# A two-layer decoder trunk on eight cores: all loads of x go through the queue of the weights, and the mixing of three token groups stands before the last two arrive

## The chip, the cores and the metric

The kernel runs on the 8 cores of one Trainium2 chip, each with its own share of the batch: one prompt of 2048 tokens and 16 running sequences with 8 new tokens each, so 2176 tokens of width 1024 a core. No core waits for another. The metric is the device time of the slowest core, in microseconds.

## The reference

```python
def trunk(x, c, pool_buf, ...):
    for i in range(DEPTH):                               # 2 layers
        sh1, sc1, g1, sh2, sc2, g2 = ada_modulation(c, w_ada[i], b_ada[i])   # silu(c) @ w_ada + b_ada
        h = modulate(x, norm_g[i, 0], sh1, sc1)          # rms_norm(x, g) * (1 + sc) + sh
        if i % N_MIXERS == 0:
            y, nb = pool_mixer(h, buf, pos0, w_pool[j], pool_scale[j])
        else:
            y, vr = sgu_mixer(h, ...)
        x = x + g1 * y
        h = modulate(x, norm_g[i, 1], sh2, sc2)
        x = x + g2 * channel_mlp(h, mlp_w1[i], mlp_w2[i])   # relu(h @ w1)**2 @ w2, width 4096
    return rms_norm(x, final_g), ...
```

The pool mixer takes, for each of four groups of 256 channels, the mean over the last 2, 4, 8 or 16 tokens less the token itself, and multiplies it by the group's 256x256 matrix. Layer 0 is a pool layer, layer 1 a gating layer.

## The kernel before

Tokens are the free dimension and channels the partitions: xT_sb holds all of x in float32 as 8 chunks of 128 channels, hT_sb the normed input in bf16. Tokens go in five groups GR of 384, 512, 512, 384 and 384; the last 128 are the running sequences. In the text x0 to x4 are the loads of these groups, 4096 bytes for each token, 8.9 MB in all.

Weights come as pieces of 2 MB of float32 in HBM, written as 1 MB of bf16 into a ring of NRING = 6 slots, in the order of the list PIECES. "ada a" is the piece of 512 columns of w_ada of layer 0: a = 2, 3 the scale of the mixer, 4, 5 its gate, 8, 9 and 6, 7 scale and shift of the MLP, 10, 11 its gate, 0, 1 the shift of the mixer. The piece wpool is 1 MB, written as float32. Pieces are issued on the queue of GpSimd (POOL), one after the other (load_piece, L545; the DMA is L558, for wpool L554). A piece waits for a free slot: until the last reader of the piece before it in the slot is done. Two pieces wait for a load of x too (GATE, L543): the first one for x2, ada 8 for x4. The loads of x are issued on SP's queue (load_x, L520).

The steps at the start, for a group g: pool_z (L713) takes the squares (ScalarE, L618), sums them over channels by a matmul with ones (L621), makes the reciprocal root (L632, L635), and multiplies x by it into hT_sb (z_ops, VectorE, L643). pool_P (L730) makes the sums over 4, 8 and 16 tokens for the upper channels. pool_mm (L759) multiplies (L793): 48 matmuls of the group's width, and the residual goes into xT_sb (resid, L690), which needs ada 4 and 5. The weights of this product are w_pool times the scale of the mixer, in two versions: 16 copies on ScalarE (L822) into a ring slot of their own, wA, which is held until the last pool_mm. They need wpool and ada 2 and 3. h2_prompt (L835) makes the second norm of the group, and affine (L647) applies scale and shift (ada 8, 9, 6, 7). ada_piece (L575) is 32 matmuls of 17 columns and an addition on VectorE (L590). Then mlp(0) starts: for each block of 512 hidden units mm1 (L951, with w1) and mm2 (L977, with w2) over the five groups. The running sequences are mixed within block 0 (sample_pool, L852).

The order of instructions on each engine is not that of the text. A planner (Sched, L88) collects all operations with a cost and a priority (S.base, or S.clk, which advances by the cost of matmuls) and places one at a time: of each engine's ready operations the one of lowest priority value that can start first, and of the engines the earliest:

```python
cands.sort(key=lambda c: (c[0], c[1]))   # time, then the engine's place in
ENGS = ("pe", "act", "dve", "pool", "sp")
```

It keeps a time for the DMA engines (DMA_RATE, DMA_LAT), in which loads follow each other. "after" orders two operations in the plan without a wait on the chip. A ring slot is given to the operation that is placed first. On the chip each engine runs its list in the planned order and waits on semaphores.

Of the kernel before, what the change touches and what calls it, by code (L numbers as in the profile page):

```python
# [18 lines left out]
GR = [(0, 384), (384, 512), (896, 512), (1408, 384), (1792, 384)]  # L19
# [4 lines left out]

ENGS = ("pe", "act", "dve", "pool", "sp")
LAT = {"pe": 0.16, "act": 0.28, "dve": 0.24, "pool": 0.3, "sp": 0.3}
DMA_RATE = 300.0e3
DMA_LAT = 2.2
TABLE_BIAS = 2.5

PIECES = [("ada", 0, a) for a in (2, 3)] + [("wpool", 0, 0)] + [("ada", 0, a) for a in (4, 5, 8, 9, 6, 7)] \
    + [("w1", 0, 0), ("ada", 0, 10), ("ada", 0, 11), ("w2", 0, 0), ("ada", 0, 0), ("ada", 0, 1)]
for _b in range(1, 8):
    PIECES += [("w1", 0, _b), ("w2", 0, _b)] + [("ada", 1, a) for a in range(2 * (_b - 1), min(12, 2 * _b))]
PIECES += [(w, 1, h) for w in ("inu", "inv", "out") for h in range(2)]
PIECES += [(w, 1, b) for b in range(8) for w in ("w1", "w2")]
# [363 lines left out]
def build_program():  # L400
    nc = bass.Bass("TRN2", target_bir_lowering=False)
    S = Sched(nc)
# [76 lines left out]
    def vcol(c, n=1):  # L479
        return vecs.ap()[:, c:c + n]  # L480
# [18 lines left out]
    def MK(l, v, dc0=0, n=8):  # L499
        return (("modT", l, v), dc0, dc0 + n)  # L500

    def hb(g):
        return GR[g][0] + 16 * (g + 1)
# [4 lines left out]
    def XK(t0, t1, dcs=range(8)):  # L508
        return [(("xT", dc), t0, t1) for dc in dcs]
# [7 lines left out]
    S.op("dve", lambda e: e.memset(hT.ap()[:, :, 0:16], 0.0), writes=HK(0, 16), cost=0.3)  # L517
    xoff = [8 * t0 for (t0, n) in GR]

    def load_x(g, after=()):  # L520
        t0, n = GR[g]
        S.op("sp", lambda e: e.dma_start(
            out=xT.ap()[:, :, t0:t0 + n], in_=d_xp.ap()[:, 8 * t0:8 * t0 + 8 * n].rearrange("p (c t) -> p c t", t=n)),
            writes=XK(t0, t0 + n), stream="s_x%d" % g, cost=0.1, nbytes=4096 * n, after=after)

    for g in range(3):
        load_x(g)
    S.op("act", lambda e: e.activation(out=siluT.ap(), in_=vcol(VCT, 136).rearrange("p (a b) -> p a b", b=NSEQ), func=AF.Silu),
         reads=VR, writes=[("siluT", 0, 1)], table="silu", cost=0.4)
    S.op("dve", lambda e: e.tensor_scalar(out=vcol(VFG, 8), in0=vcol(VFG, 8), scalar1=float(np.sqrt(D)), scalar2=None, op0=ALU.mult),  # L530
         reads=VR, writes=VR)
    S.op("dve", lambda e: e.tensor_scalar(out=vcol(VN, 32), in0=vcol(VN, 32), scalar1=float(np.sqrt(D)), scalar2=None, op0=ALU.mult),
         reads=VR, writes=VR)
# [3 lines left out]


    piece_vb = {}
    prev = [None]  # L540
    S.base = -5.0

    GATE = {("ada", 0, 2): 2, ("ada", 0, 8): 4}  # L543

    def load_piece(i):  # L545
        key = PIECES[i]
        v = S.vb("ring")
        piece_vb[key] = v
        gate = []
        if key in GATE:  # L550
            t0, n = GR[GATE[key]]
            gate = XK(t0, t0 + n)
        if key[0] == "wpool":
            n = S.op("pool", lambda e, v=v: e.dma_start(out=ring[v.slot].ap().bitcast(F32), in_=d_wp.ap()),  # L554
                     writes=[(v.key, 0, 1)], stream="w%d" % i, cost=0.53, vbs=[v], nbytes=1 << 20,
                     after=[prev[0]] if prev[0] is not None else [])
        else:
            n = S.op("pool", lambda e, v=v, i=i: e.dma_start(out=ring[v.slot].ap(), in_=d_wpk.ap()[i]),  # L558
                     reads=gate, writes=[(v.key, 0, 1)], stream="w%d" % i, cost=0.53, vbs=[v], nbytes=1 << 21,
                     after=[prev[0]] if prev[0] is not None else [])  # L560
        prev[0] = n

# [2 lines left out]
    def load_upto(key):  # L565
        k = PIECES.index(key)
        while nloaded[0] <= k:
            load_piece(nloaded[0])
            nloaded[0] += 1
# [5 lines left out]
    def ada_piece(l, a):  # L575
        key = ("ada", l, a)
        load_upto(key)
        pvb = piece_vb[key]
        v = S.vb("ps")
        mms = []  # L580
        for jj in range(4):
            for dc in range(NDC):
                mms.append((lambda e, jj=jj, dc=dc: e.matmul(  # L583
                    P_(v)[:, jj * 32:jj * 32 + NSEQ], pv(key, 512)[:, dc, jj * 128:(jj + 1) * 128], siluT.ap()[:, dc, :],
                    start=(dc == 0), stop=(dc == NDC - 1)), [(pvb.key, 0, 1), ("siluT", 0, 1)], NSEQ))
        ch = S.chain(mms, v, vbs=[pvb])
        vi, dc0 = (a * 4) // 8, (a * 4) % 8
        dst = modT.ap()[:, l, vi, dc0:dc0 + 4, :]
        bb = vcol(VBA + l * 48 + a * 4, 4)
        ev = S.op("dve", lambda e: e.tensor_tensor(  # L590
            out=dst, in0=P_(v)[:, 0:128].rearrange("p (a b) -> p a b", b=32)[:, :, 0:NSEQ], in1=bcast(bb, [1, 4], [0, NSEQ]), op=ALU.add),
            reads=[(v.key, 0, 1)] + VR, writes=[MK(l, vi, dc0, 4)], cost=0.3, vbs=[v])
        S.evac(ch, ev)
        gcol = None
        if vi in (1, 4):
            gcol = vcol(VN + (l * 2 + (0 if vi == 1 else 1)) * 8 + dc0, 4)
        elif vi == 2 and l == 0:
            gcol = vcol(VPS + dc0, 4)
        if gcol is not None:
            S.op("dve", lambda e: e.tensor_tensor(out=dst, in0=dst, in1=bcast(gcol, [1, 4], [0, NSEQ]), op=ALU.mult),  # L600
                 reads=[MK(l, vi, dc0, 4)] + VR, writes=[MK(l, vi, dc0, 4)], cost=0.3)

    sqi = [0]

# [154 lines left out]
    def pool_mm(g):  # L759
# [6 lines left out]
        for dco in range(NDC):  # L766
# [30 lines left out]
            for nd in resid(0, 2, v, dco, t0, n, 0, 0):  # L797
                S.evac(ch, nd)

    for a in (2, 3):  # L800
        S.base = 34.0
        ada_piece(0, a)
    load_upto(("ada", 0, 5))
    S.base = -5.0
    load_x(3, after=[prev[0]])
    load_x(4, after=[prev[0]])
    for g in range(5):
        S.base = [5.0, 12.0, 20.0, 53.0, 62.0][g]
        pool_z(g)
    S.base = 14.0  # L810
    pool_P(0)
    S.base = 25.0
    pool_P(1)
    S.base = 26.0
    wpv = piece_vb[("wpool", 0, 0)]
    Ap = bcast(modT.ap()[:, 0, 1, 0, 0:1], [NSEQ, 8])
    for q in range(2):
        S.op("dve", lambda e, q=q: e.tensor_tensor(out=Aw.ap()[:, q * 8:q * 8 + 8], in0=Ap, in1=vcol(VCW + 8 * q, 8), op=ALU.mult),
             reads=[MK(0, 1)] + VR, writes=[("Aw", q, q + 1)], cost=0.17)
    for k in range(8):  # L820
        for q in range(2):
# [3 lines left out]
                scale=Aw.ap()[:, q * 8 + k:q * 8 + k + 1]),  # L825
                reads=[(wpv.key, 0, 1), ("Aw", q, q + 1)], writes=[(wAvb.key, q * 8 + k, q * 8 + k + 1)],
                cost=c_act(256), vbs=[wpv, wAvb])
    for a in (4, 5):
        S.base = 50.0
        ada_piece(0, a)  # L830
    for a in (8, 9, 6, 7):
        S.base = 70.0
        ada_piece(0, a)

    def h2_prompt(g, base):  # L835
        t0, n = GP[g]
        S.base = base
        R, RK = stats(t0, n)
        z_ops(hb(g), t0, n, R, RK)
        affine(0, 1, hb(g), n, "act" if g < 3 else "dve")  # L840

    cl = [51.0, 60.0, 70.0, 80.0, 90.0]
    for g in range(5):
        S.base = cl[g]
        pool_mm(g)
        h2_prompt(g, cl[g] + 3.0)
        if g + 2 < 5:
            S.base = cl[g] + 4.0
            pool_P(g + 2)


    def sample_pool():  # L852
# [6 lines left out]
        H4 = arB(HH, 8 * 16 * 23).rearrange("p (c b j) -> p c b j", c=8, j=23)  # L859
        S.op("pool", lambda e: e.dma_start(out=arB(HH, 2944), in_=d_spT.ap()),  # L860
             writes=[AR(HH, HH + 5888)], stream="s_sp", cost=0.53, nbytes=1507328)
        S.base = 120.0
        for a in (0, 1):
            ada_piece(0, a)

# [1 line left out]
             reads=[("zl", 0, 1), MK(0, 1)], writes=[("zl", 0, 1)], cost=0.35)  # L867
# [480 lines left out]
```

How the kernel before makes its waits and increments, by code:

```python
                def body(eng, ops=seq[e], e=e):  # L351
                    for n in ops:
                        ins = None
                        for (emit, w) in n.swaits:
                            for d in w:
                                eng.wait_ge(d.sigval[0], d.sigval[1])
                            ins = emit(eng)
                        if n.stream is not None:
                            ins.then_inc(n.sigval[0], 16)
                        elif n.sig:
                            ins.then_inc(n.sigval[0], 1)
                    if e == "sp":
                        for (sem, val) in final:
                            eng.wait_ge(sem, val)
                        for e2 in ENGS:
                            if e2 != e and cnt[e2] > 0:
                                eng.wait_ge(esem[e2], cnt[e2])
```

## Time and profile before

| | |
|---|---|
| time, median of 3 runs | 1322.47 us (1322.31 to 1326.92) |
| the profiled execution | 1323.73 us, span of its slowest core 1322.2 us |
| spans of the 8 cores | 1315.9 to 1322.2 us |
| TensorE busy | 1255.1 us (95%) |
| VectorE busy | 765.4 us (58%) |
| VectorE's residual step (L690), 728 in all | 638 ns each on average |
| ScalarE busy | 587.5 us (44%) |
| DMA, mean over the span | 69 GB/s written on chip, 145.43 MB read from HBM |

Busy time is the time in which an instruction of the engine runs. Times in the trace count from the first instruction of the core. Matmuls overlap: one of 384 columns shows as 326 ns, while the next one starts half as long after it, so the pace is read from groups of them. All rows are of core 3, the slowest.

### The profile page before, as it was taken

How to read it: one execution, taken by the hardware profiler on the slowest of the kernel's cores; microseconds unless marked ns; L12 is line 12 of the kernel's file. 1: busy time of each engine (PE TensorE's matmuls, PEld its weight loads, DVE VectorE, ACT ScalarE, POOL GpSimd, SP SyncE). 2: the span in 40 equal slices, each digit the busy share in tenths (PEclk: the TensorE clock that was granted, in tenths of full speed). 3: DMA queues.
4: the chain of work that ended last, by engine and by line, in shares of the span. 5: the costliest groups of instructions: out<-in, count | busy, mean ns of one | idle time of the engine just before them, and what ended most of it. 6: DMA issues, size and time to landing. Idle time of an engine off the chain costs nothing.

```text
span 1322.2 us, 21660 instructions; the slowest of 8 cores (1315.9 to 1322.2 us)
## 1 busy us (share of the span) xinstructions
PE 1255.1 (95%) x7558; PEld 670.3 (51%) x7558; DVE 765.4 (58%) x1478; ACT 587.5 (44%) x1088; POOL 45.2 (3%) x87
## 2 busy tenths in 40 slices
PE   3299999999999999999999999999999999999995
PEld 0156565555555555555444444554545555554543
DVE  4287856545445454577657657854545445454567
ACT  5349443433333333466443555533333333333474
POOL 0001000000000000000000000000000000000000
PEclk9999999999999999999999999999999999999998
DMA  9999936434243342502000016511303031100024
GB/s 256 193 151 171 152 53 118 92 63 96 52 78 65 64 80 49 96 1 45 20 1 1 1 32 120 105 33 32 59 7 64 1 64 29 36 1 0 1 108 164
DMA packets 23880, 91.08 MB, mean 69 GB/s; under 512 B 2768, under 2 KB 10192, under 8 KB 15696
## 3 DMA queue, kind: packets, MB, share of 16 engines
q0 software_dynamic: 9392, 67.34, 28.7%
q1 hardware_dynamic: 14384, 22.35, 5.6%
q8 instruction: 65, 1.06, 0.3%
q14 instruction: 39, 0.32, 0.1%
HBM read 145.43 MB, written 11.01 MB: 118 GB/s over the span
## 4 chain that ended last, share of the span: by engine, by line
PE 89%; DMA 5%; ACT 2%; DVE 2%; issue 1%; POOL 0%; SPq 0%; DVEq 0%; ACTq 0%; POOLq 0%
PE ps L977 35%; PE ps L951 34%; PE ps L1126 5%; PE ps L1097 4%; PE ps L1213 4%; PE ps L793 2%; DMA ring<-w_pack 2%; PE ps L621 2%; DMA xT_sb<-x_pack 2%; ACT hT_sb L653 1%; PE ps L583 1%; PE ps L1128 1%; DVE xT_sb L1253 1%; DMA arena<-ln_b 1%; PE ps L1179 1%
## 5 line engine op out<-in xcount | busy, mean ns | idle before, releaser
L690 DVE SCALAR_TENSOR_TENSOR xT_sb<-ps,modT,xT_sb 128x512 f32<-128x512 f32 (+3 forms) x728 | 459.0, 638 | 440.5 <-PE ps L977 393.5
L977 PE MATMUL ps<-arena,ring 128*128 128x384 bf16 (+3 forms) x2624 | 521.7, 343 | 0.1
L951 PE MATMUL ps<-hT_sb,ring 128*128 128x384 bf16 (+2 forms) x2592 | 519.7, 345 | 0.0
L957 ACT ACTIVATE arena<-ps 128x384 bf16<-128x384 f32 (+3 forms) x324 | 169.6, 527 | 497.4 <-PE ps L951 497.3
L977 PEld LDWEIGHTS ps<-arena,ring 128*128 128x128 bf16 x2624 | 253.9, 98 | 215.6 <-issue 0.6
L951 PEld LDWEIGHTS ps<-hT_sb,ring 128*128 128x128 bf16 x2592 | 251.2, 98 | 216.2
L959 ACT ACTIVATE arena<-arena 128x384 bf16<-128x384 bf16 (+3 forms) x324 | 180.6, 561 | 28.8 <-ACT arena L957 2.2
L618 ACT ACTIVATE sq<-xT_sb 128x384 bf16<-128x384 f32 (+3 forms) x216 | 105.8, 530 | 72.1 <-DVE xT_sb L690 42.1
L643 DVE TENSOR_TENSOR hT_sb<-xT_sb,rstd 128x768 bf16<-128x768 f32 (+2 forms) x80 | 75.4, 1005 | 38.9 <-ACT rstd L635 38.8
L621 PE MATMUL ps<-sq,ones 128*128 128x384 bf16 (+3 forms) x216 | 49.0, 355 | 23.0 <-ACT sq L618 20.9
L1126 PE MATMUL ps<-ring,hT_sb 128*128 128x512 bf16 x272 | 67.2, 392 | 2.6 <-ACT arena L1102 2.6
L558 POOL DMA_DIRECT2D ring<-w_pack x62 | 33.6, 542 | 925.9 <-PE ps L951 335.2
L1097 PE MATMUL ps<-hT_sb,ring 128*128 128x384 bf16 (+1 forms) x320 | 61.3, 347 | 0.0
L1213 PE MATMUL ps<-arena,ring 128*128 128x384 bf16 (+1 forms) x320 | 60.0, 347 | 0.0
L583 PE MATMUL ps<-siluT,ring 128*128 128x17 bf16 x768 | 23.1, 172 | 26.8 <-DMA ring<-w_pack 26.5
L1213 PEld LDWEIGHTS ps<-arena,ring 128*128 128x128 bf16 x320 | 31.0, 98 | 27.8 <-issue 0.7
L1097 PEld LDWEIGHTS ps<-hT_sb,ring 128*128 128x128 bf16 x320 | 31.0, 98 | 27.4 <-issue 0.7
L621 PEld LDWEIGHTS ps<-sq,ones 128*128 128x128 bf16 x216 | 20.9, 98 | 47.3 <-issue 32.7
L653 ACT ACTIVATE hT_sb<-hT_sb,modT 128x512 bf16<-128x512 bf16 (+2 forms) x64 | 41.6, 734 | 2.9 <-DVE modT L590 2.0
L1133 ACT ACTIVATE arena<-ps 128x512 f32<-128x512 f32 x34 | 20.2, 596 | 50.4 <-PE ps L1128 45.1
L1126 PEld LDWEIGHTS ps<-ring,hT_sb 128*128 128x128 bf16 x272 | 25.2, 100 | 34.2 <-issue 9.9
L703 DVE TENSOR_TENSOR xT_sb<-xT_sb,arena 128x128 f32<-128x128 f32 x136 | 38.6, 286 | 6.8 <-DVE arena L700 0.5
(91 smaller groups left out, 467.6 us busy)
## 6 DMA issues: line engine op xcount, KB each, us to landing
ring<-w_pack POOLq DMA_DIRECT2D x62, 1024.0 KB, 9.0
xT_sb<-x_pack SPq DMA_DIRECT2D x3, 1536.0 KB, 21.6
xT_sb<-x_pack SPq DMA_DIRECT2D x2, 2048.0 KB, 18.9
y_pack<-xT_sb SPq DMA_DIRECT2D x8, 512.0 KB, 2.8
y_pack<-xT_sb SPq DMA_DIRECT2D x8, 384.0 KB, 2.5
ring<-w_pool POOLq DMA_DIRECT2D x1, 1024.0 KB, 24.1
y_pack<-xT_sb SPq DMA_DIRECT2D x4, 256.0 KB, 3.1
arena<-sp_pack POOLq DMA_DIRECT2D x1, 736.0 KB, 23.1
```

Source lines behind the costliest of these rows:

```text
L618: S.op("act", lambda e, si=si, dc=dc: e.activation(out=sqt.ap()[:, si * 512:si * 512 + n], in_=xT.ap()[:, dc, t0:t0 + n], func=AF.Square), ...
L621: mms.append((lambda e, si=si, dc=dc: e.matmul(P_(v)[:, 0:n], ones.ap(), sqt.ap()[:, si * 512:si * 512 + n], start=(dc == 0), stop=(dc == ...
L643: S.op("dve", lambda e, d=d: e.tensor_tensor(out=hT.ap()[:, d:d + step, c0:c0 + n], in0=xT.ap()[:, d:d + step, t0:t0 + n], in1=rb(R, step) ...
L653: S.op("act", lambda e, hs=hs, dc=dc: e.activation(out=hs, in_=hs, func=AF.Identity, bias=mcol(l, vS, dc), scale=mcol(l, vA, dc)), reads=r ...
L690: nodes.append(S.op("dve", lambda e: e.scalar_tensor_tensor(out=xs, in0=P_(v)[:, 0:n], scalar=mcol(l, vG, dco), in1=xs, op0=ALU.mult, op1= ...
L951: mms = [(lambda e, dc=dc: e.matmul(P_(v)[:, 0:n], pv(key, 512)[:, dc, fc * 128:(fc + 1) * 128], hT.ap()[:, dc, c0:c0 + n], start=(dc == 0 ...
L957: ev = S.op("act", lambda e: e.activation(out=av, in_=P_(v)[:, 0:n], func=AF.Relu), reads=[(v.key, 0, 1)], writes=ak, cost=c_act(n), vbs=[v])
L959: S.op("act", lambda e: e.activation(out=av, in_=av, func=AF.Square), reads=ak, writes=ak, cost=c_act(n) + 0.03)
L977: mms.append((lambda e, fc=fc, av=av: e.matmul(P_(v)[:, 0:w], pv(key, 1024)[:, fc, dco * 128:(dco + 1) * 128], av, start=(fc == 0), stop=( ...
L1097: mms = [(lambda e, dc=dc, key=key, fc=fc, v=v: e.matmul(P_(v)[:, 0:n], pv(key, 512)[:, dc, (fc % 4) * 128:(fc % 4 + 1) * 128], hT.ap()[:, ...
L1126: mms = [(lambda e, dc=dc, key=key, v=v: e.matmul(P_(v), hT.ap()[:, dc, c0:c0 + 128], pv(key, 512)[:, dc, :], start=(dc == 0), stop=False) ...
L1213: mms.append((lambda e, cc=cc, uv=uv, key=key, dco=dco, v=v: e.matmul(P_(v)[:, 0:n], pv(key, 512)[:, cc, (dco % 4) * 128:(dco % 4 + 1) * 1 ...
```

## The change

DMA_RATE of the planner goes from 300 to 315 GB/s. load_x issues on the POOL queue, in one sequence with the pieces: x0 and x1 first, x2 before ada 8, x3 and x4 before ada 10. The gates of pieces on x are gone. In PIECES w1 and w2 of block 1 come before or between ada 0 and 1 of layer 0, and ada 0 and 1 of layer 1 directly behind. The order of the text and the priorities are new: pool_z and pool_P of a group come together (zp), pool_mm of groups 0, 1 and 2 stands before zp of groups 3 and 4, and pool_mm of 3 and 4 comes last. The affine step of the second norm is on VectorE for all groups (before: ScalarE for 0 to 2). The additions behind ada pieces of layer 0 have their own priority. ada 0 and 1 of layer 0 are due at 130, not 120, ada 10 and 11 at 98, not 108, and the clock of the MLP starts at 82, not 93.

```diff
--- before.py
+++ after.py
@@ -24,13 +24,14 @@
 
 ENGS = ("pe", "act", "dve", "pool", "sp")
 LAT = {"pe": 0.16, "act": 0.28, "dve": 0.24, "pool": 0.3, "sp": 0.3}
-DMA_RATE = 300.0e3
+DMA_RATE = 315.0e3
 DMA_LAT = 2.2
 TABLE_BIAS = 2.5
 
 PIECES = [("ada", 0, a) for a in (2, 3)] + [("wpool", 0, 0)] + [("ada", 0, a) for a in (4, 5, 8, 9, 6, 7)] \
-    + [("w1", 0, 0), ("ada", 0, 10), ("ada", 0, 11), ("w2", 0, 0), ("ada", 0, 0), ("ada", 0, 1)]
-for _b in range(1, 8):
+    + [("w1", 0, 0), ("ada", 0, 10), ("ada", 0, 11), ("w2", 0, 0), ("w1", 0, 1), ("ada", 0, 0), ("ada", 0, 1), ("w2", 0, 1),
+       ("ada", 1, 0), ("ada", 1, 1)]
+for _b in range(2, 8):
     PIECES += [("w1", 0, _b), ("w2", 0, _b)] + [("ada", 1, a) for a in range(2 * (_b - 1), min(12, 2 * _b))]
 PIECES += [(w, 1, h) for w in ("inu", "inv", "out") for h in range(2)]
 PIECES += [(w, 1, b) for b in range(8) for w in ("w1", "w2")]
@@ -517,14 +518,20 @@
     S.op("dve", lambda e: e.memset(hT.ap()[:, :, 0:16], 0.0), writes=HK(0, 16), cost=0.3)
     xoff = [8 * t0 for (t0, n) in GR]
 
-    def load_x(g, after=()):
+    prev = [None]
+
+    def queue(node):
+        prev[0] = node
+
+    def load_x(g):
         t0, n = GR[g]
-        S.op("sp", lambda e: e.dma_start(
+        queue(S.op("pool", lambda e: e.dma_start(
             out=xT.ap()[:, :, t0:t0 + n], in_=d_xp.ap()[:, 8 * t0:8 * t0 + 8 * n].rearrange("p (c t) -> p c t", t=n)),
-            writes=XK(t0, t0 + n), stream="s_x%d" % g, cost=0.1, nbytes=4096 * n, after=after)
-
-    for g in range(3):
-        load_x(g)
+            writes=XK(t0, t0 + n), stream="s_x%d" % g, cost=0.53, nbytes=4096 * n, after=[prev[0]] if prev[0] is not None else []))
+
+    S.base = -5.0
+    load_x(0)
+    load_x(1)
     S.op("act", lambda e: e.activation(out=siluT.ap(), in_=vcol(VCT, 136).rearrange("p (a b) -> p a b", b=NSEQ), func=AF.Silu),
          reads=VR, writes=[("siluT", 0, 1)], table="silu", cost=0.4)
     S.op("dve", lambda e: e.tensor_scalar(out=vcol(VFG, 8), in0=vcol(VFG, 8), scalar1=float(np.sqrt(D)), scalar2=None, op0=ALU.mult),
@@ -537,26 +544,23 @@
 
 
     piece_vb = {}
-    prev = [None]
     S.base = -5.0
 
-    GATE = {("ada", 0, 2): 2, ("ada", 0, 8): 4}
+    XBEFORE = {("ada", 0, 8): (2,), ("ada", 0, 10): (3, 4)}
 
     def load_piece(i):
         key = PIECES[i]
         v = S.vb("ring")
         piece_vb[key] = v
-        gate = []
-        if key in GATE:
-            t0, n = GR[GATE[key]]
-            gate = XK(t0, t0 + n)
+        for g in XBEFORE.get(key, ()):
+            load_x(g)
         if key[0] == "wpool":
             n = S.op("pool", lambda e, v=v: e.dma_start(out=ring[v.slot].ap().bitcast(F32), in_=d_wp.ap()),
                      writes=[(v.key, 0, 1)], stream="w%d" % i, cost=0.53, vbs=[v], nbytes=1 << 20,
                      after=[prev[0]] if prev[0] is not None else [])
         else:
             n = S.op("pool", lambda e, v=v, i=i: e.dma_start(out=ring[v.slot].ap(), in_=d_wpk.ap()[i]),
-                     reads=gate, writes=[(v.key, 0, 1)], stream="w%d" % i, cost=0.53, vbs=[v], nbytes=1 << 21,
+                     writes=[(v.key, 0, 1)], stream="w%d" % i, cost=0.53, vbs=[v], nbytes=1 << 21,
                      after=[prev[0]] if prev[0] is not None else [])
         prev[0] = n
 
@@ -586,6 +590,7 @@
         ch = S.chain(mms, v, vbs=[pvb])
         vi, dc0 = (a * 4) // 8, (a * 4) % 8
         dst = modT.ap()[:, l, vi, dc0:dc0 + 4, :]
+        keep, S.base = S.base, (-1.0 if l == 0 else S.base)
         bb = vcol(VBA + l * 48 + a * 4, 4)
         ev = S.op("dve", lambda e: e.tensor_tensor(
             out=dst, in0=P_(v)[:, 0:128].rearrange("p (a b) -> p a b", b=32)[:, :, 0:NSEQ], in1=bcast(bb, [1, 4], [0, NSEQ]), op=ALU.add),
@@ -599,6 +604,7 @@
         if gcol is not None:
             S.op("dve", lambda e: e.tensor_tensor(out=dst, in0=dst, in1=bcast(gcol, [1, 4], [0, NSEQ]), op=ALU.mult),
                  reads=[MK(l, vi, dc0, 4)] + VR, writes=[MK(l, vi, dc0, 4)], cost=0.3)
+        S.base = keep
 
     sqi = [0]
 
@@ -797,21 +803,19 @@
             for nd in resid(0, 2, v, dco, t0, n, 0, 0):
                 S.evac(ch, nd)
 
+    S.base = -5.0
+    load_upto(("ada", 0, 10))
+    S.base = 18.0
     for a in (2, 3):
-        S.base = 34.0
         ada_piece(0, a)
-    load_upto(("ada", 0, 5))
-    S.base = -5.0
-    load_x(3, after=[prev[0]])
-    load_x(4, after=[prev[0]])
-    for g in range(5):
-        S.base = [5.0, 12.0, 20.0, 53.0, 62.0][g]
+    def zp(g):
+        S.base = [5.0, 12.0, 50.0, 86.0, 91.0][g]
         pool_z(g)
-    S.base = 14.0
-    pool_P(0)
-    S.base = 25.0
-    pool_P(1)
-    S.base = 26.0
+        S.base = [14.0, 20.0, 54.0, 90.0, 95.0][g]
+        pool_P(g)
+
+    zp(0)
+    S.base = 22.0
     wpv = piece_vb[("wpool", 0, 0)]
     Ap = bcast(modT.ap()[:, 0, 1, 0, 0:1], [NSEQ, 8])
     for q in range(2):
@@ -825,11 +829,8 @@
                 scale=Aw.ap()[:, q * 8 + k:q * 8 + k + 1]),
                 reads=[(wpv.key, 0, 1), ("Aw", q, q + 1)], writes=[(wAvb.key, q * 8 + k, q * 8 + k + 1)],
                 cost=c_act(256), vbs=[wpv, wAvb])
-    for a in (4, 5):
-        S.base = 50.0
-        ada_piece(0, a)
-    for a in (8, 9, 6, 7):
-        S.base = 70.0
+    for a, b in ((4, 32.0), (5, 36.0), (8, 57.0), (9, 63.0), (6, 70.0), (7, 77.0)):
+        S.base = b
         ada_piece(0, a)
 
     def h2_prompt(g, base):
@@ -837,16 +838,23 @@
         S.base = base
         R, RK = stats(t0, n)
         z_ops(hb(g), t0, n, R, RK)
-        affine(0, 1, hb(g), n, "act" if g < 3 else "dve")
-
-    cl = [51.0, 60.0, 70.0, 80.0, 90.0]
-    for g in range(5):
+        affine(0, 1, hb(g), n, "dve")
+
+    cl = [43.0, 51.0, 61.0, 94.0, 99.0]
+    def pm(g):
         S.base = cl[g]
         pool_mm(g)
         h2_prompt(g, cl[g] + 3.0)
-        if g + 2 < 5:
-            S.base = cl[g] + 4.0
-            pool_P(g + 2)
+
+    zp(1)
+    pm(0)
+    zp(2)
+    pm(1)
+    pm(2)
+    zp(3)
+    zp(4)
+    pm(3)
+    pm(4)
 
 
     def sample_pool():
@@ -859,7 +867,8 @@
         H4 = arB(HH, 8 * 16 * 23).rearrange("p (c b j) -> p c b j", c=8, j=23)
         S.op("pool", lambda e: e.dma_start(out=arB(HH, 2944), in_=d_spT.ap()),
              writes=[AR(HH, HH + 5888)], stream="s_sp", cost=0.53, nbytes=1507328)
-        S.base = 120.0
+        S.base = 130.0
+        load_upto(("ada", 0, 1))
         for a in (0, 1):
             ada_piece(0, a)
 
@@ -1258,11 +1267,11 @@
                  reads=XK(t0, t0 + n, [d, d + 1]), stream="o_y", cost=0.1, nbytes=1024 * n)
 
     load_upto(("w1", 0, 0))
-    S.base = 108.0
+    S.base = 98.0
     ada_piece(0, 10)
     ada_piece(0, 11)
     S.base = None
-    S.clk = 93.0
+    S.clk = 82.0
     mlp(0, after=lambda g: norm(1, 0, g), hooks=hooks0, first=sample_pool)
     sgu()
     mlp(1, after=final)
```

## Rows read from the trace of the kernel before

**Rows 1.** Who TensorE waited for, 0 to 130 us: total, times, longest.
```profile
PE ps L583 <- DMA ring<-w_pack: 26.5, 3, 10.6
PE ps L621 <- ACT sq L618: 18.3, 3, 12.0
```

**Rows 2.** TensorE in order of time: start, us, line, [idle before <-releaser].
```profile
25.74 4.22 PE L621 MATMUL ps<-sq,ones 128*128 128x512 bf16 x8 [2.96 <-ACT sq L618]
...
46.84 1.01 PE L583 MATMUL ps<-siluT,ring 128*128 128x17 bf16 x32 [5.39 <-DMA ring<-w_pack]
58.46 1.01 PE L583 MATMUL ps<-siluT,ring 128*128 128x17 bf16 x32 [10.61 <-DMA ring<-w_pack]
59.31 0.48 PE L793 MATMUL ps<-hT_sb,ring 128*128 128x384 bf16 x1
```

**Rows 3.** Stretches: length, busy us by engine, granted clock, DMA share, GB/s written.
```profile
10.00:25.00 15.00, 7.48 (x16) 1.65 (x16) 6.76 (x14) 11.31 (x22) 0.00 (x0) 1.00 1.01 310
...
59.00:65.00 6.00, 6.00 (x45) 3.13 (x42) 1.83 (x5) 1.69 (x5) 0.00 (x0) 1.00 0.79 192
...
80.00:150.00 70.00, 68.98 (x552) 39.62 (x551) 60.76 (x104) 54.54 (x109) 4.83 (x9) 1.00 1.01 170
```

**Rows 4.** Loads of x: SP's issues, the chain, and microseconds from issue to landing.
```profile
1.52 5.10 SPq L522 DMA_DIRECT2D xT_sb<-x_pack  x3
6.66 6.68 SPq L855 DMA_DIRECT2D npsTa<-sp_tail  x1
...
2.60 22.28 DMA xT_sb<-x_pack
...
xT_sb<-x_pack SPq DMA_DIRECT2D x1, 1536.0 KB, 9.6
npsTa<-sp_tail SPq DMA_DIRECT2D x1, 448.0 KB, 19.6
...
65.59 2.12 POOL L558 DMA_DIRECT2D ring<-w_pack  x4 [37.30 <-DMA xT_sb<-x_pack]
```

**Rows 5.** Two pieces of weights, three loads apart: issues, then us to landing.
```profile
91.82 0.54 POOL L558 DMA_DIRECT2D ring<-w_pack  x1 [20.37 <-PE ps L583]
...
110.57 0.54 POOL L558 DMA_DIRECT2D ring<-w_pack  x1 [5.77 <-PE ps L583]
...
ring<-w_pack POOLq DMA_DIRECT2D x1, 1024.0 KB, 16.6
...
ring<-w_pack POOLq DMA_DIRECT2D x1, 1024.0 KB, 16.7
```

**Rows 6.** TensorE's pace: mixing at its start, later at 512 and 384 columns, ada.
```profile
59.69 1.44 PE L793 MATMUL ps<-hT_sb,ring 128*128 128x384 bf16 x4
...
84.69 4.49 PE L793 MATMUL ps<-hT_sb,ring 128*128 128x512 bf16 x20
...
98.85 4.07 PE L793 MATMUL ps<-hT_sb,ring 128*128 128x384 bf16 x24
...
129.39 1.77 PE L583 MATMUL ps<-siluT,ring 128*128 128x17 bf16 x64
```

**Rows 7.** ScalarE in order of time: squares and norm of x2, the copies to wA.
```profile
24.96 4.27 ACT L618 ACTIVATE sq<-xT_sb 128x512 bf16<-128x512 f32 x8 [0.68 <-DMA xT_sb<-x_pack]
...
30.90 0.63 ACT L635 ACTIVATE rstd<-rstd 128x512 f32<-128x512 f32 x1
50.90 6.48 ACT L822 ACTIVATE ring<-ring,Aw 128x256 bf16<-128x256 f32 x16 [19.38 <-DMA ring<-w_pool]
```

**Rows 8.** Pooled sum of x1, multiplication of x2, the affine step on both engines.
```profile
30.03 1.25 DVE L738 TENSOR_TENSOR arena<-hT_sb 128x2108 bf16<-128x2108 bf16 x1
...
32.56 4.62 DVE L643 TENSOR_TENSOR hT_sb<-xT_sb,rstd 128x1024 bf16<-128x1024 f32 x4
...
119.60 5.74 ACT L653 ACTIVATE hT_sb<-hT_sb,modT 128x512 bf16<-128x512 bf16 x8
...
132.70 2.40 DVE L656 TENSOR_SCALAR hT_sb<-hT_sb,modT 128x384 bf16<-128x384 bf16 x8
```

## The prediction

> **What bounds the kernel now.** I read four views in this order. First, who TensorE waited for in the first 130 us: only loads of w_pack (26.5 us) and the squares of the statistics (18.3 us) [rows 1]. Over the whole span it is busy 1255 of 1322 us, so nearly all its idle time lies in this start. Second, its own instructions in order of time: three statistics, three ada pieces, and from 59.3 us the first mixing matmul, behind ada 4, whose load lands at 58.3 [rows 2]. From there to 130 us TensorE has under 1 us of idle time: whatever is done before 59.3 us moves the end, and little else does. Third, the stretches: the DMA share is 1.0 from 10 to 25 us at 310 GB/s written (x, float32) and from 80 to 150 us at 170 GB/s written (weights, read as float32 and written as bf16, so 340 read) [rows 3]. So the start is set by how many bytes stand ahead of ada 4. Fourth, the landings: x0 at 1.52+9.6 = 11.1 us, x2 at 24.9, the copy to npsTa at 6.66+19.6 = 26.2, x4 only by 65.6, where it releases ada 8, because x3 and x4 share the engines with the pieces [rows 4].
>
> **The order of loads.** Before, everything of x (8.9 MB) is ahead of or beside ada 4. After, only x0 and x1 are. I count a ladder of landings. x0 and x1: what was landed at 26.2 less the time of x2; x0 to x2 is 13.8 us for two groups of 512 [rows 4], with the copy beside one of them, so 6.5 each: 19.7 us. A piece of weights: issued at 91.82 and 110.57 they land at 108.4 and 127.3, three pieces apart, so 6.3 us each [rows 5]. w_pool is half of that in bytes read: 3.2 (between ada 3 and the copies that it releases the rows have 4.1 us, with x4 beside it [rows 2, 7]). Then ada 2 at 26.0, ada 3 32.3, w_pool 35.5, ada 4 41.8, ada 5 48.1, x2 54.6, ada 8 60.9, ada 9 67.2, ada 6 73.5, ada 7 79.8, w1 block 0 at 86.1, x3 91, x4 96, ada 10 102, ada 11 109, w2 block 0 at 115. The copy to npsTa now stands at the very start on SP, which has only vecs before it; its time is inside the 19.7.
>
> **The pool queue.** x2 to x4 now stand in one queue with pieces that wait for ring slots. Six slots are filled at once by ada 2, ada 3, w_pool, ada 4, ada 5, ada 8. ada 9 waits for TensorE's ada 2 (27 us), ada 6 for ada 3 (33 us), and behind them stand w1, x3 and x4. The data ahead of them covers this: when ada 7 is issued (about 49 us) x2, ada 8, ada 9 and ada 6 are still to be moved, 25 us of work. Were a slot to come later than 73 us, x3 and x4 would be late by the difference. I cost it at nothing. An issue on this queue is 0.54 us with VectorE fully busy beside it [rows 5]; five more are 2.7 us on an idle engine. For x one issue has 1024 short runs in place of 128 rows, which no row shows on this queue; between nothing and one load time (6.5 us, once, since later issues lie beside data) I take under 1, as the issues on record do.
>
> The Trainium skill (DMA: Bandwidth & Descriptors, Issuing engine by pattern) says the sync queue is generally faster than the GpSimd one; its section Latency and other measured facts has about 1 against 0.6 us to the first byte. By it the sum would be some 0.4 us worse, once. The trace neither supports nor denies it for x, as no x goes by that queue.
>
> **The start of the mixing.** The scaled weights wA need a ring slot and w_pool. The planner's list gives a slot that comes free to ACT before POOL at equal times; the slots of ada 2 and 3 go to ada 9 and 6 before wA is ready, so wA gets that of ada 4, at 42.9 (landing 41.8 and 0.9 for the chain). The 16 copies take 6.48 us [rows 7]; a first chain needs four: 1.6. So the first mixing matmul runs at about 45.0, not 59.3. The work of TensorE done until then is 3 ada pieces in both cases, and 2 statistics in place of 3: 8 times 0.216 = 1.7 us move behind the start. Net 59.3-45.0-1.7 = 12.6 us.
>
> **Does TensorE stay fed until w1?** From 45.0 to 86.1 are 41.1 us. The full-rate costs are 0.163 us for 384 columns (3.9 over 24) and 0.216 for 512, and 0.87 for an ada piece [rows 6]. Mixing of group 0: 48 matmuls, 7.8 and 0.6 for the short ones; groups 1 and 2: 10.4 each; five ada pieces 4.3; one statistic of x2 and three of the second norm 6.5 (1.7+1.3+1.7+1.7). Together 40.0. At its start TensorE runs slow: the 384-column matmuls from 59.7 us are some 0.31 apart, which is 1.2 GHz by their pace although the granted clock reads 1.00, after ten idle microseconds; from 65 us the pace is 0.163, 2.4 GHz [rows 3, 6]. That cost 2.3 us before and I take the same after, so it cancels, but it belongs in the fit: 42.3 us of work in 41.1. So work and arrival nearly meet. x2 must be in: landing 54.6, squares 4.3, norm 2.3 (29.23 to 31.53), multiplication 4.6, pooled sums 3.2 (two of 1.25 and one over half the channels, 0.7) = 69 us [rows 7, 8], and VectorE also has 16 residuals of 0.64 and 3.5 us of the second norm of group 0 in there, 14 us: say 72. TensorE has until then 8.4+10.4 for groups 0 and 1, three ada, three statistics (4.7) and 2.3 = 28.4, to 73. It fits barely. The last statistic of group 2 can't run before w1 lands (its residual and squares come behind the mixing at 84), so I charge 1.0 us of idle time at 85. Gain 11.6 us.
>
> The same as lost time, that is time less work at full rate: before, 59.3 less 4.7 for three statistics and 2.6 for three ada pieces, plus 2.3, is 54.3. After, it can't be less than w1's landing less all that fits before it: 86.1-45.6 = 40.5, where 45.6 is the 40.0 above with two statistics and three ada pieces; the forecast is 42.7.
>
> **After w1.** The first MLP halves of groups 0 to 2 are 5.2+6.9+6.9 = 19.0 us, to about 106, in which x3 and x4 (91 and 96) are squared, normed and summed by 102 to 107; then 7.8 and 5.2 of mixing, and w2 is there (115). No arrival binds here. VectorE: the affine step of groups 0 to 2 goes from ScalarE (5.74 us for a 512 group) to VectorE (2.40 for a 384 group, about 2.8 for 512): 8 us more [rows 8]. It was busy 60.8 of 70 us from 80 to 150 [rows 3]; over 45 to 150 us it now has some 85 us of work in 105, and ScalarE loses 16 us. Hidden as long as no single stretch exceeds it; from 86 to 125 I count 43 us of work for it in 39 (multiplications 4.6 for group 2 and twice 6.1 for groups 3 and 4, pooled sums 4.3, 24 residuals 14, affine 7.5), of which the last 10 (second norm of groups 3 and 4) are not needed before 130. If that cover fails, up to 5 us. The order of the later pieces (w1 and w2 of block 1 earlier, ada 0 and 1 later) is free: they land by 127 to 140 and are needed from about 165.
>
> **Sum.** The profiled execution took 1323.7 (span 1322.2). 1323.7-11.6 = 1312.1; it stands 1.3 above the median of 1322.5, so 1311.
>
> **The rivals.**
> A. The start comes early but less is kept: wA gets ada 5's slot (start 51.1, gain 59.3-51.1-1.7+0.9 = 7.4, 1315), or x goes by this queue at w_pool's pace of 4.1 us a MB: x0 to x2 take 23.6 in place of 19, w1 lands at 91, and lost time is 91-45.6 = 45.4 for 54.3: gain 8.9, 1314. For it: the only float32 load on this queue shows that pace. Against: x4 ran beside it. With VectorE's 5 us on top, 1318 to 1320.
> B. The saved time is wholly given back: TensorE comes earlier to the same work but then waits in its fixed order, for x2's sums at 72, w1 at 86 and VectorE at 110, because the planner's times for copies (0.29 planned, 0.40 measured) and for the slow clock are too short. Each wait that costs 4 us or more; 1318 to 1325. Against: the same planner left under 1 us of waits from 59.3 on. But then everything had long landed.
> C. Slower: the pool queue moves x no faster than it writes weights, 166 GB/s written. x0 to x2 then take 35 us and not 19, w1 lands at 102, lost time is 102-45.6 = 56.4 for 54.3: 1325, and with x3 and x4 late as well 1328. It decides below about 180 GB/s for x. Against: the limit of weights seems to be what is read, 340 GB/s, and w_pool made 256 written.
> D. More gain: x2's sums on time, no idle time at 85, loads at 6.0 us: bounded by w1's landing, 84-45.6 = 38.4 lost for 54.3: 1307.
>
> **How the numbers follow.** The forecast with D 0.55, A 0.22, B 0.15, C 0.08. A change under 0.5% (6.6 us) can't be told from none here. Faster (below 1315.9): forecast and D, and the better half of A and a little of B, 0.70. Same: 0.21. Slower (above 1329) 0.09 with C and accidents. The range 1303 to 1320 holds the forecast, D and nearly all of A, and a part of B.
>
> **What would show it.** ada 4 should land near 42 us and the first mixing matmul run near 45; x1 near 19.7 (later than 23 speaks for C); w1 block 0 near 86; x4 near 96; mixing of group 2 over by 84. TensorE's idle time before the first mixing matmul falls from about 45 to some 32 us and from then to 130 us is under 3 us; if its waits for VectorE or for w_pack come to over 5 us after 45 us, B. The rest of the kernel, from about 170 us on, should be the same and some 11 us earlier. The prediction is wrong if wA's copies start at 49 us or later, or if TensorE's slow pace returns in gaps after 50 us.

## The result, and the profile after

The changed kernel takes 1330.16 us (median of 5 runs, 1329.1 to 1331.1) where the kernel before takes 1322.95 (5 runs beside it). The ratio is 1.0051 with a 95% interval of 1.0040 to 1.0062: slower by some 7 us, where 1311 was forecast. The profiled execution is itself of 1330.16 us; the span of its slowest core, core 6, is 1328.6.

The early part went as forecast. TensorE of core 6 in order of time, with what ended the idle time before:

```profile
43.81 1.00 PE L587 MATMUL ps<-siluT,ring 128*128 128x17 bf16 x32 [8.81 <-DMA ring<-w_pack]
45.67 0.48 PE L799 MATMUL ps<-hT_sb,ring 128*128 128x384 bf16 x1 [0.86 <-ACT ring L826]
...
88.62 2.82 PE L960 MATMUL ps<-hT_sb,ring 128*128 128x384 bf16 x16 [1.28 <-DVE xT_sb L696]
...
194.77 1.66 PE L627 MATMUL ps<-sq,ones 128*128 128x128 bf16 x8 [6.93 <-ACT sq L624]
```

Ada 4 runs at 43.8 and the first mixing matmul at 45.7 us (forecast 45.0), where it was at 59.3 [rows 2]. The first MLP matmul is at 88.6, w1's load having been issued at 54.77 and having taken 33.7 us, so in at 88.5 (forecast 86.1). The last line is what the prediction did not have on its list: before the statistic of the 128 tokens of the running sequences TensorE stands still for 6.9 us. The same view of the kernel before, where it did not wait:

```profile
194.49 0.61 PE L621 MATMUL ps<-sq,ones 128*128 128x128 bf16 x8
```

The stretches of core 6 (columns as in [rows 3]):

```profile
65.00:140.00 75.00, 69.09 (x529) 38.38 (x533) 67.09 (x121) 41.27 (x86) 4.96 (x9) 0.98 0.99 186
...
187.00:195.00 8.00, 1.07 (x8) 0.46 (x5) 2.67 (x5) 0.69 (x4) 0.00 (x0) 0.73 0.48 62
195.00:205.00 10.00, 9.95 (x55) 5.11 (x56) 7.27 (x10) 5.02 (x14) 0.00 (x0) 0.71 0.17 54
150.00:165.00 15.00, 14.95 (x91) 8.77 (x90) 8.20 (x12) 5.17 (x11) 0.00 (x0) 1.00 0.01 2
```

From 65 to 140 us TensorE is idle for 5.9 us (1.0 on core 3 of the kernel before); the granted clock falls behind the stall (0.73 and 0.71 in 187 to 205 us), so for 10 us it works partly at 1.2 GHz; and from 150 to 165 us the DMA engines do next to nothing (a share of 0.01).

What holds the statistic? The chain of work of core 6 and the instructions of POOL, SP and VectorE on it:

```profile
165.27 1.77 PE L587 MATMUL ps<-siluT,ring 128*128 128x17 bf16 x64
...
166.77 0.53 POOL L562 DMA_DIRECT2D ring<-w_pack  x1 [33.22 <-PE ps L587]
167.58 0.53 POOL L562 DMA_DIRECT2D ring<-w_pack  x1 [0.28 <-issue]
...
168.98 23.25 DMA npsb_pack<-arena
...
192.33 1.29 DVE L932 TENSOR_TENSOR arena<-ps,modT 128x512 f32<-128x512 f32 x2 [12.97 <-DMA npsb_pack<-arena]
```

Ada 0 and 1 of layer 0 are in at 128 to 135 us, but the plan runs them at 165. They free two ring slots, so POOL issues two loads of weights at 166.8 and 167.6. The same ada pieces let VectorE finish the new pooling state, which SP stores to npsb_pack from the buffer H3 at 169.0. The store lands 23.3 us later, and L932 writes its product into H3 and has to wait for that, then the residual, the squares, the statistic. In the kernel before the same store, its issue and its time to landing:

```profile
154.52 0.38 SPq L880 DMA_DIRECT2D npsb_pack<-arena  x1
```

```profile
DMA to landing us min/median/max: 20.4/20.4/20.4
```

It is in at 174.9, 20 us ahead of its statistic. On core 1 of the changed kernel the store takes 18.9 us and TensorE waits 2.6; the even cores wait 6 to 7 us. Hence spans of 1317 to 1322 on the odd cores and 1324 to 1329 on the even ones, where those before are 1315.9 to 1322.2. That it is the even cores holds for this execution only: in two others cores 3 (1326.0), 1 (1324.5) and 5 (1324.2) are among the late ones.

**Lost time.** To add this up I use the measure of the prediction: the time less TensorE's work done until then, columns at 2.4 GHz as in [rows 6], summed over all its matmul records. One core with complete records for each kernel, the slowest such or, for oldclk, loads and store1st, one within 2.2 us of it:

| kernel, core | span | lost at 65 us | 140 | 180 | 210 | 500 |
|---|---|---|---|---|---|---|
| before, 3 | 1322.2 | 54.4 | 55.8 | 55.7 | 55.6 | 55.1 |
| changed, 4 | 1327.0 | 43.3 | 51.1 | 52.8 | 62.3 | 61.8 |
| t4, 2 | 1335.9 | 43.3 | 50.9 | 52.6 | 66.0 | 72.3 |
| b120, 7 | 1324.4 | 42.6 | 50.2 | 53.4 | 59.1 | 58.6 |
| t4b120, 3 | 1318.0 | 43.1 | 50.5 | 50.6 | 52.4 | 51.9 |
| aff, 4 | 1328.4 | 43.3 | 53.7 | 55.4 | 64.6 | 64.0 |
| b105, 1 | 1314.3 | 43.1 | 50.5 | 50.6 | 50.7 | 50.2 |
| t4b105, 1 | 1313.8 | 42.2 | 49.9 | 49.8 | 49.6 | 49.1 |
| oldclk, 1 | 1315.7 | 42.4 | 49.6 | 52.2 | 52.2 | 51.7 |
| loads, 3 | 1339.5 | 41.1 | 63.3 | 75.7 | 75.5 | 75.1 |
| store1st, 3 | 1323.2 | 42.6 | 50.3 | 51.9 | 61.2 | 60.8 |
| b105aff3, 3 | 1313.6 | 42.6 | 48.1 | 48.8 | 48.7 | 48.3 |

At 65 us the change is 11.1 us ahead; at 140 us 4.7 (7.8 lost on the way, 1.4 before); at 180 us 2.9; at 210 us it is 6.7 behind. The rows below it are the experiments.

### The profile page after: what moved, and what is told of

It is laid out like the page before. It is cut to its first block, busy times and chain, and to the rows that moved or that the text cites. A ratio compares the mean times of both kernels' runs of the same rounds, so it can differ in the third digit from the quotient of the medians.

```text
span 1328.6 us, 21584 instructions; the slowest of 8 cores (1317.3 to 1328.6 us)
## 1 busy us (share of the span) xinstructions
PE 1252.9 (94%) x7463; PEld 670.8 (50%) x7558; DVE 772.2 (58%) x1502; ACT 574.1 (43%) x1064; POOL 49.6 (4%) x92
## 4 chain that ended last, share of the span: by engine, by line
PE 89%; DMA 5%; DVE 2%; issue 2%; ACT 1%; POOL 0%; DVEq 0%; ACTq 0%; SPq 0%; POOLq 0%
PE ps L986 34%; PE ps L960 34%; PE ps L1135 5%; PE ps L1106 4%; PE ps L1222 4%; DMA ring<-w_pack 3%; PE ps L799 3%; PE ps L627 2%; DMA npsb_pack<-arena 2%; PE ps L587 1%; PE ps L1137 1%; DVE xT_sb L1262 1%; DVE hT_sb L662 1%; PE ps L1188 1%; ACT sq L624 0%
## 5 line engine op out<-in xcount | busy, mean ns | idle before, releaser
L696 DVE SCALAR_TENSOR_TENSOR xT_sb<-ps,modT,xT_sb 128x384 f32<-128x384 f32 (+3 forms) x728 | 458.3, 638 | 435.9 <-PE ps L986 388.6
L960 PE MATMUL ps<-hT_sb,ring 128*128 128x384 bf16 (+2 forms) x2542 | 518.5, 345 | 6.7 <-DVE xT_sb L696 3.6
L1135 PE MATMUL ps<-ring,hT_sb 128*128 128x512 bf16 x262 | 64.1, 386 | 3.6 <-ACT arena L1111 3.0
L799 PE MATMUL ps<-hT_sb,ring 128*128 128x384 bf16 (+2 forms) x157 | 37.7, 352 | 1.7 <-ACT ring L826 0.9
L706 DVE TENSOR_TENSOR arena<-ps,modT 128x128 f32<-128x128 f32 x136 | 38.2, 283 | 0.4 <-PE ps L986 0.3
```

Of the source, the lines that this page charges most:

```text
L696: nodes.append(S.op("dve", lambda e: e.scalar_tensor_tensor(out=xs, in0=P_(v)[:, 0:n], scalar=mcol(l, vG, dco), in1=xs, op0=ALU.mult, op1= ...
L799: mms.append((lambda e, kind=kind, k=k, ap=ap, nn=nn, i=i, W=W, v=v, m=len(lst): e.matmul(P_(v)[:, 0:nn], W(kind, k), ap, start=(i == 0), ...
L960: mms = [(lambda e, dc=dc: e.matmul(P_(v)[:, 0:n], pv(key, 512)[:, dc, fc * 128:(fc + 1) * 128], hT.ap()[:, dc, c0:c0 + n], start=(dc == 0 ...
L1135: mms = [(lambda e, dc=dc, key=key, v=v: e.matmul(P_(v), hT.ap()[:, dc, c0:c0 + 128], pv(key, 512)[:, dc, :], start=(dc == 0), stop=False) ...
```

## The experiments

All are edits of the changed kernel except "loads". The planner sets the order anew for each, so an edit can move more than itself: TensorE's order parts from that of the changed kernel at 102 us in aff, at 139 in b105, at 153 in b120 and at 182 in t4 and store1st. Each ratio is to the kernel before, run beside that version.

**t4: the product away from the store's buffer.**

```diff
-            tk = [AR(H3 + hf * 2048, H3 + hf * 2048 + 2048)]
-            t4 = arF(H3 + hf * 2048, 512).rearrange("p (c b t) -> p c b t", c=4, t=8)
-            t3 = arF(H3 + hf * 2048, 512).rearrange("p (c t) -> p c t", t=128)
+            tk = [AR(HH + hf * 2048, HH + hf * 2048 + 2048)]
+            t4 = arF(HH + hf * 2048, 512).rearrange("p (c b t) -> p c b t", c=4, t=8)
+            t3 = arF(HH + hf * 2048, 512).rearrange("p (c t) -> p c t", t=128)
```

> The changed kernel, with the product of the running sequences' mixing written over the state buffer HH in place of H3, so that it no longer waits for the store npsb_pack out of H3. Theory S (the stall is the wait for that store, which stands behind two loads of weights): the 13 us wait of VectorE (L932) and the 6.9 us of TensorE at 187 us are gone and so is the slow pace after it (3 us); the wait of the slower cores falls to under 1 us, all cores end within 5 us of each other, median 1320 to 1322. Rival L (the path is late whatever it waits for, since ada 0 and 1 run at 165 us): TensorE still waits 3 us or more before the statistic of 128 columns, median 1326 or more.

Measured: 1337.56 us, ratio 1.0115 (1.0099 to 1.0131), worse than the change. Both theories missed. The wait for the store is gone from L932, and the statistic runs without a wait; the store is then waited for by something else. SP, VectorE and TensorE of core 2:

```profile
167.86 1.42 SPq L889 DMA_DIRECT2D npsb_pack<-arena  x1
...
193.10 0.34 SPq L1079 DMA_DIRECT2D arena<-bsp_pack  x1
193.53 0.57 SPq L1077 DMA_DIRECT2D arena<-wsp_pack  x1
...
212.95 1.10 DVE L1083 TENSOR_TENSOR arena<-arena 128x256 bf16<-128x256 f32 x3 [20.23 <-DMA arena<-wsp_pack]
...
214.39 1.01 PE L986 MATMUL ps<-arena,ring 128*128 128x128 bf16 x8 [17.68 <-DVE arena L706]
```

The load of bsp_pack goes into memory that the store still reads, so SP holds it until the store is in, at 193.0; wsp_pack is behind it in SP's queue and takes 19.3 us more; and VectorE, in its fixed order, has the product with wsp_pack (L1083) ahead of residuals that TensorE needs. Three cores (3, 4 and 7), on which the store was in by 184.5 to 186.8, waited only 1.0 to 2.2 us there and have spans of 1315 to 1316; the other five, where it came at 190 to 193, have 1332 to 1336. So what a late store costs depends on the waiter that it meets, and here the second one was dearer than the first.

**b120: ada 0 and 1 due at 120, as before the change.**

```diff
-        S.base = 130.0
+        S.base = 120.0
         load_upto(("ada", 0, 1))
```

> The changed kernel with the base of ada 0 and 1 of layer 0, and what follows on it, back at 120 in place of 130. They then stand about 12 us of TensorE's work earlier, the store too. Theory S, in its form that the store takes some 20 us wherever it is and must only start early enough: landing at about 177, before TensorE needs the statistic; stall under 1 us, median 1320 to 1322, as with the buffer moved. Rival L says the same for this run. A third theory, that the even cores are slow in themselves (their spans 1324 to 1329 against 1317 to 1322), leaves 4 us or more between even and odd cores.

Measured: 1328.61 us, ratio 1.0041 (1.0027 to 1.0055). The store is issued at 157.5 on core 0, 11 us earlier, but takes 24.4 us, and the planner has moved the statistic earlier with it: TensorE waits 7.1 us at 177 to 184. An earlier store helps only if its waiter does not come with it.

**t4b120: both.**

> Both: the product in HH and the base at 120. If the stall is all there is behind 150 us, this is no faster than either alone, 1320 to 1322; if each removed only a part, it is faster than both by 1 us or more.

Measured: 1319.29 us, ratio 0.9984 (0.9961 to 1.0006), which the interval does not tell from the kernel before, and 9 us below b120 and 18 below t4: the second of the expected cases. Its executions differ: two of the nine compared end at 1327.5 and 1328.2, each with one late core, the others at 1316.6 to 1321.9. The statistic runs at 176.1 without a wait; VectorE still waits 7.4 us for wsp_pack on core 0, TensorE 3.2 for that.

**aff: the affine step of groups 0 to 2 back on ScalarE.**

```diff
-        affine(0, 1, hb(g), n, "dve")
+        affine(0, 1, hb(g), n, "act" if g < 3 else "dve")
```

> The changed kernel with the affine step of groups 0 to 2 on ScalarE, as before the change. Theory V (the waits of TensorE between 85 and 140 us, some 6 us more than at 65 us, come from VectorE, which has 8 us more to do there): lost time between 85 and 140 us falls by 3 us or more; but the stall at 187 stays, median about 1326 to 1328. Rival W (those waits are of ScalarE's squares, interleaved with the MLP's activations, and of the planner's order): no gain or a loss of 1 to 4 us, 1330 to 1334.

Measured: 1332.57 us, ratio 1.0078 (1.0056 to 1.0099). Lost time at 140 us is 53.7 and not 51.1; TensorE now waits 2.2 us for the affine step on ScalarE. Giving VectorE this work was right for the stretch up to 140 us, and theory V falls in this form; the new order from 102 us on is part of what was measured.

**b105 and t4b105: ada 0 and 1 as soon as they are in.** As b120 with 105.0; t4b105 with the edit of t4 too.

> The base of ada 0 and 1 at 105, the product still in H3, behind the store. If the store takes some 20 us wherever it is, it is in by 165 us, before the statistic of 128 columns: as good as with the product in HH, 1316 to 1318. If it is short in an empty queue (a few us), the same. If the planner now places the statistic right behind it, part of the wait comes back, 1320 to 1325.

> The product in HH and the base of ada 0 and 1 at 105, so that they run as soon as they are in (128 and 135 us), and the store npsb_pack goes out near 145, where the DMA queues run empty (150 to 165 us in the changed kernel). Theory S: no wait over 1 us behind 145 us on any core, lost time stays near 51 from 140 us to 500 us, as against 55 before; spans of all cores 1308 to 1316, median 1316 to 1318, and the spread between even and odd cores under 5 us. Rival E (the even cores lose in themselves): spread as in the changed kernel, and no better than the run with both at 120 (1319.3).

Measured: b105 1316.22 us, ratio 0.9958 (0.9942 to 0.9974); t4b105 1315.86, ratio 0.9956 (0.9943 to 0.9969), 6 us faster than the kernel before. SP and TensorE of core 1 in b105 in order of time, and then the stretch of core 6 in which the changed kernel stood still:

```profile
146.48 0.67 SPq L889 DMA_DIRECT2D npsb_pack<-arena  x1
...
175.93 0.61 PE L627 MATMUL ps<-sq,ones 128*128 128x128 bf16 x8
```

```profile
187.00:195.00 8.00, 8.00 (x80) 4.92 (x78) 7.66 (x26) 2.45 (x4) 0.53 (x1) 1.00 0.83 137
```

The store still takes 22.2 us, in at 168.6, and nobody waits for it: L932 is at 171.0. One number, the due time of two ada pieces, is worth 14 us by the two medians and 12 to 13 by what each kernel differs from the kernel before beside it. Even and odd cores now end within 4 us (1310.6 to 1314.3), so rival E falls.

**oldclk: the due times of before the change.**

```diff
-    S.base = 98.0
+    S.base = 108.0
     ada_piece(0, 10)
...
-    S.clk = 82.0
+    S.clk = 93.0
```

with ada 0 and 1 at 120.

> The changed kernel with the due times of before: MLP clock 93, ada 10 and 11 at 108, ada 0 and 1 at 120. Theory S with the due times as its cause: relative to the MLP's clock the path of the running sequences is where it was before (27 in place of 48 units behind), so the stall at 187 us is gone; but pool mixing goes before MLP work from 94 on, which is right for the start. 1318 to 1322. If the stall stays over 3 us, the due times are not the cause but that TensorE is 10 us ahead of the same DMA work.

Measured: 1318.40 us, ratio 0.9972 (0.9961 to 0.9983). The store is issued at 147.7, the statistic waits 0.6 us on core 0 and 1.5 on core 1. The distance between the MLP's clock and the due time of ada 0 and 1 had been 27 and became 48; put back to 27, most of the stall is gone.

**loads: the kernel before with the loads alone changed.** x on the POOL queue in the new order, no gates; nothing else.

> The kernel before with the loads alone changed: x on the POOL queue in the new order (x2 before ada 8, x3 and x4 before ada 10), the gates gone; old order of the text, old pieces, old due times, affine of groups 0 to 2 on ScalarE. If the early start (ada 4 at 43 us, first mixing matmul near 46 where it was 59) is the work of the order of loads alone, it shows here, lost time near 43 at 65 us. Then the planner's old order decides: kept to 140 us better than in the changed kernel, 1314 to 1318; or given back as there, 1320 to 1330.

Measured: 1343.20 us, ratio 1.0160 (1.0146 to 1.0175), outside what was expected. The first mixing matmul is at 45.9 us and lost time at 65 us 41.1, so the early start is the work of the order of loads alone. TensorE of core 6 then:

```profile
93.21 3.26 PE L621 MATMUL ps<-sq,ones 128*128 128x384 bf16 x8 [9.29 <-ACT sq L618]
```

In the old order the statistic of x3, which now lands at 92 us, stands ahead of work that is ready: 9.3 us idle here, 2.5 at 96 and 5.2 at 155. The other half of the change (mixing of three groups and MLP work ahead of x3 and x4, with the new due times, pieces and affine step, which were not taken apart here) is what keeps the start: it is worth 12 us at 140 us (63.3 against 51.1).

**store1st: the store alone in the queues.** The next load of weights waits until the store is in.

```diff
-                     writes=[(v.key, 0, 1)], stream="w%d" % i, cost=0.53, vbs=[v], nbytes=1 << 21,
+                     reads=[("store", 0, 1)] if key == ("ada", 1, 0) else [], writes=[(v.key, 0, 1)], stream="w%d" % i, cost=0.53, vbs=[v], nbytes=1 << 21,
...
-        S.op("sp", lambda e: e.dma_start(out=o_npsb.ap(), in_=arF(H3, 1024)), reads=hk, stream="o_m3", cost=0.1, nbytes=524288)
+        S.op("sp", lambda e: e.dma_start(out=o_npsb.ap(), in_=arF(H3, 1024)), reads=hk, writes=[("store", 0, 1)], stream="o_m3", cost=0.1, nbytes=524288)
```

> The changed kernel (base 130, product in H3), with one wait added: the first load of weights behind ada 0 and 1 waits until the store npsb_pack has landed. TensorE's order is then that of the run with the product in HH. Theory Q (the store's 20 to 25 us are the two loads of weights of 6 us each that the same ada pieces release 2 us before it, not the store's own time): it lands within 6 us, the waits of VectorE for it (13 us at 179) and for the load of wsp_pack (20 us) are under 2 us, all cores within 6 us, lost time stays near 51 to 53, median 1317 to 1321. Rival O (a store of 512 KB into HBM takes this long by itself here): it lands after 18 us or more, the waits stay, and the loads that wait behind it make it 1330 or more.

Measured: 1328.02 us, ratio 1.0049 (1.0034 to 1.0064). TensorE's order is that of t4. On core 0 SP's issue of the store; POOL's issue of the two loads, now behind it; the time from issue to landing of the store; and VectorE and TensorE in order of time:

```profile
166.80 0.34 SPq L889 DMA_DIRECT2D npsb_pack<-arena  x1
```

```profile
176.68 1.06 POOL L562 DMA_DIRECT2D ring<-w_pack  x2 [43.44 <-DMA npsb_pack<-arena]
```

```profile
DMA to landing us min/median/max: 9.4/9.4/9.4
```

```profile
201.94 1.10 DVE L1083 TENSOR_TENSOR arena<-arena 128x256 bf16<-128x256 f32 x3 [10.27 <-DMA arena<-wsp_pack]
...
203.38 1.01 PE L986 MATMUL ps<-arena,ring 128*128 128x128 bf16 x8 [7.73 <-DVE arena L706]
```

The store is in after 9.4 us (7.6 to 10.3 over the eight cores) in place of 23.0 on this core of the changed kernel (18.0 to 23.3 over its eight), so 9 to 15 us of it, core by core, were the two loads ahead. The expected 6 us were too few; the small copy to npp_pack stands 1.1 us ahead of it on SP and takes as long, and what the rest of the time is was not tried. The wait of L932 is gone. But the two loads, now later, stand ahead of wsp_pack, which is issued at 187.6 and takes 14.2 us, and the wait moves to L1083 (10.3 us): theory Q holds for the cause and misses in the time.

**b105aff3: the affine step of group 3 on ScalarE, on top of b105.**

```diff
-        affine(0, 1, hb(g), n, "dve")
+        affine(0, 1, hb(g), n, "act" if g == 3 else "dve")
```

> The run with the base of ada 0 and 1 at 105, with the affine step of group 3 on ScalarE, which is idle at 130 to 135 us, where TensorE waits 2 us for residuals behind VectorE's multiplication and affine step of group 3. If VectorE's order is what makes that wait: it falls by 1.5 to 2.5 us, and with the slow pace behind it the end by 2 to 3: 1313 to 1314. If the affine step is then late on ScalarE behind the activations: no change, 1316.

Measured: 1315.05 us, ratio 0.9948 (0.9935 to 0.9961). The wait of 2 us that begins at 133 us is gone and lost time at 140 us is 48.1 in place of 50.5, as expected. The end gains only about 1 us on b105, which its interval does not separate. By its median it is the fastest version here, 7 us below the kernel before.

## Why the prediction was wrong

**Right: the ladder of loads and the start.** Landings came 1 to 3 us late along the whole ladder (ada 4 at 43.7 for 41.8, ada 8 at 64.1 for 60.9, w1 at 88.5 for 86.1), wA took ada 4's slot, the copies began at 45.0 and the mixing at 45.7. The lead at 65 us is 11.1 us; the forecast had 12.6 there, and 11.6 only behind the idle time at 85 us, so 1.5 us are missing, about what ada 4 came late. x on the POOL queue was as fast as on SP's (x2 is in at 55.7, 5.8 us behind ada 5, where two such loads took 13.8 on SP): rival C did not happen, nor the slow form of A. The two issues of x0 and x1 took 1.96 us together, 0.98 each in place of 0.54, inside the "under 1".

**Mis-sized: the idle time behind the start.** The 1.0 us charged at 85 us was 1.3 on core 6. But from 65 to 140 us the changed kernel loses 7.8 us where the one before loses 1.4; the forecast had nothing there beyond the 1.0. Of these, 2 us are the wait from 133 to 135 us that b105aff3 removed with some 0.4 more behind it. The largest others on core 6 are waits of 0.3 to 1.3 us that end at 73, 81, 89, 92 and 106 us, and statistics whose eight matmuls each wait a little for a square (2.1 us for the eight at 101.6 us, 1.5 where none waits), while ScalarE is fully busy from 95 to 110 us with squares between activations of the MLP. This is rival B in its place though not in its size; that ScalarE is the cause in 95 to 110 us is read from the trace and was not tested. One of the prediction's own signs of being wrong did come: on core 6 the granted clock is 0.66 in 135 to 140 us, behind that wait of 2 us, and 0.71 in 195 to 205; on core 4 it stays at 1.00 from 65 to 140 us behind the same wait.

**Wrong: "The order of the later pieces (w1 and w2 of block 1 earlier, ada 0 and 1 later) is free: they land by 127 to 140 and are needed from about 165".** Ada 0 and 1 landed as said, by 135.5 (w2 of block 1 stands behind them as it did before the change, and landed at 142.0; only w1 of block 1 was moved ahead of them). But 165 was when the plan ran them, not when they were needed. What hangs on them is a chain through SP's store of some 20 us, and it was counted at nothing; on that rests the sentence that the rest of the kernel, from about 170 us on, "should be the same and some 11 us earlier". Behind 180 us the kernel lost 9.5 us in that place: 6 to 7 of waiting and 3 of slow pace behind it. b105 gave back the whole of it by starting the chain when its data were in, and t4, store1st and t4b120 show that removing one waiter or shortening the store alone only moves the wait to the next one. The prediction had read the change of the due time from 120 to 130 and priced neither it nor the clock's from 93 to 82, which together put TensorE's work 21 units of the planner's time further ahead of that chain.

Added up from the table, before and changed: the forecast was 11.6 us less lost and the measured 6.7 us more. Of the 18.3 us between, 1.5 are the start, 5.4 the stretch from 65 to 140 us, 1.8 that to 180, and 9.6 the store's chain.

Open: what is lost behind 500 us differs too. Span less lost time at 500 us is 1322.2-55.1 = 1267.1 for the kernel before, 1314.3-50.2 = 1264.1 for b105 and 1323.2-60.8 = 1262.4 for store1st. So some 3 of the 7.9 us between the spans of before and b105 arise there, and no run says why; TensorE's order in the kernel before is that of the changed kernel only from about 850 us on, and that of b105 and store1st from about 200 and 210. Why one core's store takes 23.3 us (core 6) and another's 18.9 (core 1) was not tried; in t4 the slow ones are cores 0, 1, 2, 5 and 6.

## What to carry to other kernels

A lead on the bounding engine is a debt on every chain that runs beside it: when work is pulled forward, list the side chains with a DMA in them and ask for each when its data are there, when it starts and who waits for its end. Price a store or a load by issue-to-landing in that place of the trace, not by its bytes: here 512 KB took 18 to 25 us where the instructions that released it had released two loads of weights just before, and under 10.4 where those waited. And a due time in a planner is a part of the change like any other.

## What the runs showed that was not expected

A store of 512 KB from SP took 17.4 to 26.8 us, over all cores of all runs, beside one or two loads of weights issued 1.4 to 8.1 us before it, and 7.6 to 10.3 us without them (store1st), although the loads stand in another queue: the queues share the engines. The Trainium skill (Trainium Kernel Development and Optimization, Key Constraints) says so of the queues of SP, ACT and POOL: they run on the same 16 engines and interleave. The runs agree.

A stall of 7 us at 187 us on core 6, whose TensorE had waited for no more than 0.6 us at a time since 135 us, was followed by a granted clock of 0.71 in 195 to 205 us, which cost 3 us more. On core 1, with a stall of 2.6 us, the granted clock was 0.87 from 182 to 190 us and 0.93 from 190 to 200, and some 2 us were lost behind it.
